# RWKV products over four 64x64 tiles and two banks by head parity, WU in a buffer of its own, and the next operands formed among the state products

## The reference, cut to what matters

```python
def step(S, inp):
    r_t, w_t, k_t, a_t, b_t, v_t = inp
    sa = jnp.einsum('bhvk,bhk->bhv', S, a_t)
    S = S * w_t[:, :, None, :] + sa[..., None] * b_t[:, :, None, :] + v_t[..., None] * k_t[:, :, None, :]
    return S, jnp.einsum('bhvk,bhk->bhv', S, r_t)
```

## Time and profile before

| | |
|---|---|
| median of 3 runs | 1153.89 us (1150.84 to 1157.65) |
| the profiled execution, its own time | 1155.38 us |
| its span, first to last instruction | 1153.5 us |
| TensorE busy | 937.7 us, 81% |
| VectorE busy | 587.1 us, 51% |
| ScalarE busy | 297.1 us, 26% |
| GpSimd busy | 99.2 us, 9% |
| mean granted clock of TensorE | 0.875 |

### The profile page before, as it was taken

The page is one execution under the profiler, slowest core; times in us unless marked ns, Lnnn a source line. Parts: engine busy times, 40 slices in busy tenths (PEclk is TensorE's granted clock), DMA queues, the critical chain, the costliest instruction groups (busy, mean ns, idle before and its releaser), DMA issues.

```text
span 1153.5 us, 20409 instructions
## 1 busy us (share of the span) xinstructions
PE 937.7 (81%) x8617; PEld 611.6 (53%) x8617; DVE 587.1 (51%) x1081; ACT 297.1 (26%) x506; POOL 99.2 (9%) x125
## 2 busy tenths in 40 slices
PE   2899999979949974688888877879998599999910
PEld 0455455645526543677777777744547344444400
DVE  2350157889963886666666665245634222222235
ACT  2230110300003445333333332132212022322232
POOL 4000121030020002111111110000000100000030
PEclk9899999979978975789888888979896699999965
DMA  9602332223302200222212111181117379999562
GB/s 341 251 1 85 116 113 74 74 77 121 119 31 92 64 1 12 40 39 44 40 34 39 35 36 32 26 285 40 70 37 239 108 250 369 368 369 356 182 221 97
DMA packets 140023, 142.11 MB, mean 123 GB/s; under 512 B 70925, under 2 KB 106121, under 8 KB 139913
## 3 DMA queue, kind: packets, MB, share of 16 engines
q1 hardware_dynamic: 130792, 115.09, 31.5%
q0 software_dynamic: 3744, 13.63, 3.3%
q10 hardware_dynamic: 5376, 11.86, 2.7%
HBM read 121.41 MB, written 19.15 MB: 122 GB/s over the span
## 4 chain that ended last, share of the span: by engine, by line
PE 61%; DVE 18%; issue 9%; DMA 6%; ACT 2%; SPq 1%; POOL 1%; POOLq 0%; DVEq 0%; ACTq 0%
PE bank L1684 58%; PE bank L1688 3%; DVE rk_r L1214 3%; DMA region<-in_w_out_dram 1%; ACT region L802 1%; DMA region<-in_w_ada_dram 1%; DVE cl_b L1116 1%; DMA ada_row_buffers<-a_rows_dram 1%; DMA a_rows_dram<-region 1%; DVE region L1472 1%; DMA region<-expert_rows_dram,pick_slots 1%; DVE region L1405 1%; DMA inverse_rows_dram<-ada_row_buffers 1%; DMA region<-inverse_rows_dram 1%; DVE region L1214 1%
## 5 line engine op out<-in xcount | busy, mean ns | idle before, releaser
L1684 PE MATMUL bank<-region 64*64 64x64 f32 (+3 forms) x5376 | 598.8, 320 | 86.3 <-DVE region L1405 37.9
L1684 PEld LDWEIGHTS bank<-region 64*64 64x64 f32 (+1 forms) x5376 | 384.8, 165 | 289.9 <-issue 207.1
L802 ACT ACTIVATE region<-bank 128x512 f32<-128x512 f32 (+2 forms) x212 | 112.5, 531 | 562.0 <-PE bank L1684 441.8
L1688 PE MATMUL bank<-ident,region 128*128 128x128 f32 (+2 forms) x303 | 53.7, 318 | 32.8 <-DMA gk_sb<-in_gla_gk_dram 12.5
L1661 DVE TENSOR_SCALAR region<-region 128x256 f32<-128x256 f32 x16 | 4.7, 294 | 143.2 <-ACT region L802 143.2
L1684 PE MATMUL bank<-region,rk_r 128*128 128x512 f32 x160 | 72.0, 604 | 0.0
L1688 PEld LDWEIGHTS bank<-ident,region 128*128 128x128 f32 (+2 forms) x303 | 41.0, 164 | 48.7 <-issue 24.3
L1214 DVE SCALAR_TENSOR_TENSOR rk_r<-region,vec,rk_r 128x512 f32<-128x512 f32 x64 | 54.2, 847 | 2.3
L1684 PE MATMUL bank<-vtok_b,region 64*64 64x64 f32 x960 | 48.4, 219 | 2.0 <-DVE region L1422 2.0
L1684 PEld LDWEIGHTS bank<-region,rk_r 128*128 128x128 f32 x160 | 30.2, 194 | 34.6 <-issue 34.6
L1684 PEld LDWEIGHTS bank<-vtok_b,region 64*64 64x64 f32 x960 | 46.2, 136 | 2.2 <-DVE region L1422 2.2
(11 more groups left out here) (257 smaller groups left out, 978.1 us busy)
## 6 DMA issues: line engine op xcount, KB each, us to landing
region<-in_moe_w_dram SPq DMA_DIRECT2D x36, 1024.0 KB, 9.7
region<-in_w_ada_dram SPq DMA_DIRECT2D x12, 2048.0 KB, 9.0
region<-in_w_in_dram SPq DMA_DIRECT2D x6, 2048.0 KB, 7.8
cl_b<-in_moe_w_dram SPq DMA_DIRECT2D x12, 1024.0 KB, 11.6
expert_rows_dram<-yg_b ACTq DMA_DIRECT2D x16, 512.0 KB, 7.0
region<-inverse_rows_dram SPq DMA_DIRECT2D x40, 128.0 KB, 3.1
region<-in_w_out_dram SPq DMA_DIRECT2D x2, 2048.0 KB, 13.7
a_rows_dram<-region SPq DMA_DIRECT2D x20, 128.0 KB, 2.6
```

The source lines that it names most:

```text
L802: return act.activation(out, in_, func, **kw)
L1684: return pe.matmul(out, lhsT, rhs, start=start, stop=stop)
L1688: return pe.transpose(out, in_, ident[0:n, 0:n])
```

## The change

The products of both head parities are issued alternately and go to a bank for each parity, so four quarters of the array are addressed in turn, from two banks. This holds for the scores, for `blocks` (for X5 and X6 the odd heads' D2 is stored in the other partition half, `swapped`), for the part of Y from the state, and in G and `seq` by chunk and parity. Every copy of such a product is two instructions, one for each parity. WU moves to a buffer `scratch` (which constants of earlier stages use before), so b and k need not wait for Y. `decay_exps` is split: `decays` and `k_factors` stand ahead of the WU copies, `growths` behind. `decayed` is split: `decayed_ra` after the G copies, `decayed_bk` between the two state copies, `chunk_decays` after the second, and this one gives `s_ops`. The second state product of the last two steps, whose result nothing reads, is left out. D2 is loaded by four transfers of four heads instead of two of eight.

```diff
-            g.WU = view(1024, 1024, "p (h n) -> p h n", h=NH)
+            g.WU = scratch[:, 1024 * d:1024 * (d + 1)].rearrange("p (h n) -> p h n", h=NH)
...
+        def pair(n, h):
+            return [(n, h, 0), (n, h, 1)]
...
-            return [(n, h) for n in ("b0", "A", "b1", "k0", "k1")]
+            return pair("A", h) + pair("b", h) + pair("k", h) if h % 2 == 0 else pair("b", h) + pair("A", h) + pair("k", h)
...
-                        dst = g.X1[sc] if k == 0 else g.D2[sc]
-                        sp.dma_start(dst, chunk_rows(inv_dram[2 * k + d], cp)).then_inc(s_inv[k][d], 16)
+                        sc, other = slice(cp * HD, (cp + 1) * HD), slice((1 - cp) * HD, (2 - cp) * HD)
+                        rows = chunk_rows(inv_dram[2 * k + d], cp)
+                        if k == 0:
+                            sp.dma_start(g.X1[sc], rows).then_inc(s_inv[0][d], 16)
+                        else:
+                            sp.dma_start(g.D2[sc, 0::2], rows[:, 0::2]).then_inc(s_inv[1][d], 16)
+                            sp.dma_start(g.D2[other, 1::2], rows[:, 1::2]).then_inc(s_inv[1][d], 16)
...
+                if later:
+                    decays(h + 2)
+                    k_factors(h + 2)
                 for j in range(2):
                     copy_out(g.WU[:, 4 * j:4 * j + 4], ("WU", h, j), bank(("WU", h, j))[:, :].rearrange("p (h k) -> p h k", k=2 * HD))
-                if h + 2 < NS:
-                    decay_exps(h + 2)
+                if later:
+                    growths(h + 2)
...
-                if p >= 1:
-                    wait_filled(dve, "Y", h - 2)
...
+                if later:
+                    decayed_ra(h + 2)
+                for k in range(2 if later else 1):
                     cp = chunk(d, k)
                     dst = MM[:, d] if k == 0 else MR[:, nxt, d]
                     wait_filled(dve, "seq", h, k)
                     out_of(TT(dst, bank(("seq", h, k))[:, 0:RC * HD].rearrange("p (h i) -> p h i", h=RC),
                               bc(pcs[:, d, :, cp], 2, HD), ALU.mult), "seq", h, k)
+                    if later:
+                        if k == 0:
+                            decayed_bk(h + 2)
+                        else:
+                            chunk_decays(h + 2)
...
-                turn = half_done(a_rows(0))
-                with_b(0)
-                open_bank("A", h)
-                pe.wait_ge(s_turn, turn)
-                finish(a_rows(1))
-                with_b(1)
-                with_k(0)
-                with_k(1)
...
+                def both_parities(n, width, lhsT, rhs):
+                    bs = [open_bank(n, h, 0), open_early(n, h, 1)]
                     for i in range(RC):
                         for cp in range(2):
+                            for hp in range(2):
+                                last = mm(bs[hp][half(cp), i * width:(i + 1) * width], lhsT(hp, i, cp), rhs(hp, i, cp))
...
-                b = open_bank(n, h)
-                for m in range(NH):
-                    for cp in range(2):
-                        ins = mm(b[half(cp), m * HD:(m + 1) * HD], lhsT(half(cp), m), rhs(half(cp), m))
-                finish(ins)
+            def blocks(n, h, lhsT, rhs, swapped=False):
+
+                bs = [open_bank(n, h, 0), open_early(n, h, 1)]
+                for m in range(0, NH, 2):
+                    for hp in range(2):
+                        for cp in range(2):
+                            at = 1 - cp if hp == 1 and swapped else cp
+                            to = 1 - at if hp == 1 else at
+                            last = mm(bs[hp][half(to), m // 2 * HD:(m // 2 + 1) * HD], lhsT(half(at), m + hp), rhs(half(at), m + hp))
```

More of the change, by code:

```diff
@@ L935, in _, with k_factors, decays @@
             heads = lambda v: v.rearrange("p (h k) -> p h k", k=HD)
-            def decay_exps(h):
+            def k_factors(h):
+                p, d, g, t = step(h)
+                if p == 0:
+                    act.wait_ge(s_seg, d + 1)
+                else:
+                    wait_filled(act, "tK", h - 2)
+                for i in range(RC):
+                    ins = A(g.k[:, i], aa[:, d, i, t * P:(t + 1) * P], ACT.Identity, scale=vec[:, vka + i:vka + i + 1], bias=oneka[:, i:i + 1])
+                    own(ins) if i < RC - 1 else tell(ins, s_f)
+            def decays(h):
                 p, d, g, t = step(h)
@@ L1490, in _ @@
                 nxt = 1 - MCUR[p]
-                more = h + 1 < NS
+                more, later = h + 1 < NS, h + 2 < NS
                 if more:
@@ L2013, in scores @@
-                with_b(1)
-                with_k(0)
-                with_k(1)
+                            for hp in range(2):
+                                last = mm(bs[hp][half(cp), i * width:(i + 1) * width], lhsT(hp, i, cp), rhs(hp, i, cp))
+                                if hp == 0:
+                                    evens = last
+                    finish(evens)
+                    open_bank(n, h, 1)
+                    finish(last)
+                a_part = lambda hp, i, cp: g.AR[half(hp), i, cp, 0]
@@ new lines, in back_products @@
+                for n in range(NH):
+                    for cp in range(2):
+                        ins = mm(bs[cp][half(n % 2), (n // 2) * 2 * HD:(n // 2 + 1) * 2 * HD], g.WU[half(cp), n, 0:HD], g.B3[half(cp), 1:3, n])
+                        if cp == 0:
+                            firsts = ins
+                finish(firsts)
+                open_bank("G", h, 1)
+                finish(ins)
+                ks = range(2 if h < NS - 2 else 1)
+                loaded, bs = [0, 0], [open_early("seq", h, k) for k in ks]
@@ L2071, in back_products @@
                 by_chunk = half_done(ins)
-                for k in range(2):
+                for k in ks:
                     cp = chunk(d, k)
@@ L2115, in _ @@
                 pe.wait_ge(s_inv[0][d], 32 * (p + 1))
-                wait_result(pe, "A", h)
+                for hp in range(2):
+                    wait_result(pe, "A", h, hp)
                 blocks("Z1", h, of(U1t), of(g.X1))
@@ L2119, in _ @@
                     turned("tA", h + 1)
-                pe.wait_ge(s_inv[1][d], 32 * (p + 1))
-                wait_result(pe, "Z1", h)
-                blocks("X5", h, of(g.D2), of(Z))
+                pe.wait_ge(s_inv[1][d], 64 * (p + 1))
+                for hp in range(2):
+                    wait_result(pe, "Z1", h, hp)
+                blocks("X5", h, of(g.D2), of(Z), swapped=True)
                 if more:
@@ L2125, in _ @@
                     turned("tK", h + 1)
-                wait_result(pe, "X5", h)
+                for hp in range(2):
+                    wait_result(pe, "X5", h, hp)
                 blocks("Z2", h, of(U2t), of(g.X0))
@@ L2130, in _ @@
                     scored_v(h + 1)
-                wait_result(pe, "X5t", h)
-                wait_result(pe, "Z2", h)
-                blocks("X6", h, of(g.D2), of(Z))
-                wait_result(pe, "X6", h)
+                for hp in range(2):
+                    wait_result(pe, "X5t", h, hp)
+                    wait_result(pe, "Z2", h, hp)
+                blocks("X6", h, of(g.D2), of(Z), swapped=True)
+                for hp in range(2):
+                    wait_result(pe, "X6", h, hp)
                 wait_result(pe, "tA", h)
```

256 lines of the change are left out of this document (131 added, 125 removed).

## The result

The kernel after takes 1127.49 us (median of 4 runs, 1124.13 to 1129.45) against 1154.56 for the kernel before in the same runs, a ratio of 0.9763 with a 95% interval of 0.9732 to 0.9793. The forecast was 1119, range 1102 to 1143. The profiled execution took 1129.45 us, its span is 1127.6.

The account below looks back on a forecast made before the run. TensorE, busy 81%, bounded the kernel; VectorE's list, fed by the block DMA, would take over. Gains of 43, 3 and 5.5 us sum to 51.5, less 63 x 0.26 for low clock: 35, so 1119 us, range 1102 to 1143.

Parts of the forecast that it names:

- charge of 63 x 0.26 for the clock: All nine steps at low clock would cost about 63 us; the low share was kept at 0.26.
- seven steps: RWKV steps between third and tenth: 29.16 to 23.0 us each, 6.2 gained seven times, 43 us at full clock.
- The bound moves to VectorE's list, fed by the block DMA: In each RWKV step, VectorE's work behind the 6.8 us row store and block load sets the time, not TensorE's list.
- The pause ahead of the scores: TensorE's 2.40 us idle before each step's scores was to fall under 0.5 us.
- 23.0 us a step at full clock: From one start of scores to the next, along VectorE's list and the block DMA, 23.0 us instead of 29.16.
- The low share: Share of the steps' time at half clock, f, kept at the kernel before's 0.26; gain 51.5 - 63f.
- 7 us of charge for a low step: At low clock TensorE sets the step again: WU, G, the path to X6, preloads, state products and Y add 7 us.
- The first step, 3 us: Only the end of the scan- and DMA-bound first step gains: 2.4 us of pause and 0.6 of preloads.
- The last two, 5.5 us less 3.6 of charge: Last two steps: 2.9 from earlier sixteens, 1.3 dropped state product, 0.5 Y product, 0.7 blocks; 5.5 us at full clock.
- The tiles: Four 64x64 tiles run at once, taken as 24 ns per 64-column product, bounded by 15 and 29; not on the path.
- the burst: GLA-stage products queued behind transposes on four tiles: 16 MATMULs in 0.47 us, about 15 ns each.
- D2 as four loads, "level, no spare": D2 as half loads lands 10.5 instead of 9.2 us past sixteens, just when X5 wants it; 2 us late costs 18.

Follow-up runs that it names:

- both_ends: Kernel after with blocks in two tiles, D2 by two loads, one filler ahead of WU, step 1's k factors earlier, fillers in the last step: 1111.42 us.
- blocks_two_tiles: Kernel after with Z1, X5, Z2, X5t and X6 back in two tiles and D2 loaded by two whole loads: 1123.21 us, 0.9742 of the kernel before.
- parities_apart: Kernel after with each pair of products issued one parity after the other, two tiles at a time: 1127.25 us, 0.9774 of the kernel before.
- run 32: Not a run: in "run 32 MATMULs" the word is a verb; four 64x64 tiles execute 32 MATMULs of 64 columns in 0.69 us.

## Why the prediction was right, and where its sizes were off

The direction, the mechanism and the range held; the gain was 27 us instead of 35. Taken as the forecast added it up, with its charge of 63 x 0.26 for the clock, the two profiled spans, 25.9 us apart, account for the missing 9 us like this:

| term | forecast | measured |
|---|---|---|
| first to third release | 3 | 0.1 |
| seven steps | 43 - 12.7 = 30.3 | 25.4 |
| last two steps | 5.5 - 3.6 = 1.9 | 1.2 |
| ahead of and behind these | 0 | -0.9 |

- **The bound moves to VectorE's list, fed by the block DMA: right.** VectorE waits for the blocks in all eight steps, leaving the transfer out shortened the time to the end of sixteens by 1.1 us, and at full clock the tail is VectorE's list alone: 5.69 us without a wait, 7.14 with 1.46 us of work added.
- **The pause ahead of the scores: wrong in size.** It was to fall under 0.5 us and is 1.01, down from 2.40. TensorE sits idle there until ScalarE's copies of Y and VectorE's small copy are done, which end together at about 571.4.
- **23.0 us a step at full clock: right for the undisturbed step, short for the mean.** Steps 1 and 3 took 23.01 and 22.62 us; sixteens ended 17.32 and 16.93 us after the release, where the list has 17.3. Over the seven they ended at 17.78, which costs 3.5 us; steps 2 and 5 alone cost 4.6, the others a little less than forecast. In step 2 the scores start at 522.11, 1.83 us after the release, behind the transposes of the first state (from 520.50 us on), and eights start 3 us late. The kernel before had the same transposes (from 521.52 us on), but they ran in its pause, ahead of the release at 524.80. The forecast's list had overlooked them. In step 5 the blocks came 4.47 us after the load was issued (603.97 to 608.44), in step 4 2.62 (577.27 to 579.89); no run shows why.
- **The low share: close, in part by luck.** 0.88 from third to tenth release is a share of 0.24 against the 0.26 taken. But the share had been kept for want of a row and not derived, and the low stretches now lie elsewhere, the three long ones beginning in the pause ahead of WU (at about 583.0, 610.5 and 637.5 us) and reaching into the preloads. Over the last two steps the clock was 0.79, with 0.65 in the last alone: a share of 0.42 and 0.70.
- **7 us of charge for a low step: about right in sum, wrong in its spread.** The tails are 14.1 us longer over seven steps than the forecast's 5.73, against a charge of 12.7. They are spread unevenly: a step with a long stretch (share 0.38) has a tail 3.2 to 3.7 us longer, where the formula gives 7 x 0.38 = 2.7. The stretch begins ahead of WU, so WU and G, 3.68 + 1.99 instead of 1.96 + 1.10 us, and the preloads are slow, and these are on the path. Low clock elsewhere in the step costs next to nothing: steps 1 and 3 have a share of 0.14 and 0.16 and the tail of 5.69.
- **The first step, 3 us: wrong.** It gained 0.1. The second to third release shrank by 1.2 us, of the 2.4 of pause only 1.4 could be had, and the first to second grew from 17.95 to 19.03. There the operands' chain ScalarE, GpSimd, VectorE stands behind the AV copy, as in the kernel before; moving the factors gave 1.95 back, which shows the chain. Why it is 1.1 us longer than before isn't shown; the masks, now two for each product, are my guess.
- **The last two, 5.5 us less 3.6 of charge: 0.7 short.** The sum at full clock was the better part: with fillers there, blocks on two tiles and a clock of 1.00 (both_ends) the last two took 43.6 us, 5.8 below the 49.35 before. The charge was too small, since the last step was the slowest-clocked of all; by its share of 0.42 it is 5.9.
- **The tiles.** 24 ns was taken for a 64-column product, 14 ns were measured, just under the 15 of the burst. It changed nothing on the path, as the text said.
- **D2 as four loads, "level, no spare": held.** One wait of 1.4 us, in the last step, although the sum took the shortest landing time, 3.0 us, and not the median of 3.3. Of the other figures, WU, its copies and G are given as 3.9 us from terms that add up to 3.7; rows of the kernel after have 3.9 (510.27 to 514.13).

What stays open: what lets the clock fall in one step and not in the next; what share of blocks_two_tiles' advantage is D2's earlier landing; and why the transfer of single steps takes 2 us more.

## What to carry to other kernels

When an edit speeds up an engine that is about to stop being the bound, its gain can be hidden wholly. What then sets the step is found with two or three marks on the new path: here the start of eights, the end of sixteens and the next release. Read them step by step beside the granted clock. Size the charge of low clock by the instructions that the low stretch falls on, and not by an average. Where added work seems to cost nothing, look for a step at full clock before calling the engine idle: in the median 11.7 us of work cost 4, in such a step all of it. A pause that cannot be removed can be filled with idle products into a bank that is overwritten anyway, as long as the filler is sized from a row and is shorter than the pause; the same filler cost 29 us at 7.1 us a step and gave 10 us at 1.8.

## What the runs showed of the hardware

- Four 64x64 tiles in turn run 32 MATMULs of 64 columns in 0.69 us, 14 ns each, in X5, Z2, X5t and X6 and not only in a burst queued ahead; AV, still on two tiles, takes 1.15. The Trainium skill, "TensorE: Matmul & The Clock Gate", section "Wait — 56ns, not 53.3ns?", has starts never closer than about 25 ns; these rows disagree with it for products on different tiles, in the profiler's records.
- The pauses ahead of WU that preceded half clock in the kernel after were 1.18 to 3.25 us long. In parities_apart those of 1.49 and 2.10 us preceded it and those of 2.00 and 2.58 did not. The Trainium skill, same page, section "HAM oscillation — how this bites in real kernels", describes the clock falling over waits between bursts of products, which agrees in kind.
- A 128x512 f32 MATMUL leaves two records and took 0.88 us at full clock (7.13 us for eight), four times what I had taken from the shape.
- A load of half of D2 costs SyncE as much issue as a whole one: 0.58 to 0.62 us in most rows of the kernel after for 64 KB (others up to 1.48), 1.27 for two of 128 KB.

```profile
619.31 1.27 SPq L652 DMA_DIRECT2D region<-inverse_rows_dram  x2
...
622.20 0.62 SPq L655 DMA_DIRECT2D region<-inverse_rows_dram  x1
622.86 0.62 SPq L654 DMA_DIRECT2D region<-inverse_rows_dram  x1
```
